# Where tiles start in on-chip memory: padding the shared region to multiples of 512 bytes

## The reference

```python
mod = (c_act @ w_ada[l] + b_ada[l]).reshape(B, N_SUBLAYERS, 3, D)
shift, scale, gate = mod[:, :, 0], mod[:, :, 1], mod[:, :, 2]

h = x * (1.0 + scale[:, 0, None, :]) + shift[:, 0, None, :]
y = _swiglu(h, ffn1_w_in[l], ffn1_w_out[l])          # 1024 -> 2 x 2816 -> 1024
x = _layernorm(ALPHA * x + 0.5 * gate[:, 0, None, :] * y, ...)

h = x * (1.0 + scale[:, 1, None, :]) + shift[:, 1, None, :]
proj = h @ w_in[l]
cq, ckv, k_rope_raw, u = jnp.split(proj, split_at, axis=-1)
attn = _mla(cq, ckv, k_rope_raw, positions, ...)     # 8 heads, chunk-causal
pooled = _multiscale_pool(u, pool_w[l], pool_b[l], pool_scale[l])
y = jnp.concatenate([attn, pooled], axis=-1) @ w_out[l]
x = _layernorm(ALPHA * x + gate[:, 1, None, :] * y, ...)
...                                                  # a second feed-forward like the first
```

## The kernel before

| tile | start | by 512 | by 64 | by 2,048 |
|---|---|---|---|---|
| h_hi, h_lo, x, w_hi, w_lo, raw, act_t, sums | 4,096 to 120,832 | 0 | 0 | 0 |
| ones_t, ones_d | 123,456; 123,968 | 64 | 0 | 576; 1,088 |
| gb | 124,576 | 160 | 32 | 1,696 |
| ada_first, a_hi1, a_hi2, u | 125,088 | 160 | 32 | 160 |
| w_hi_early, w_lo_early | 190,624; 198,816 | 160 | 32 | 160 |
| a_lo1, a_lo2 | 170,144 | 160 | 32 | 160 |
| c_act, ada_ring | 215,200; 219,296 | 160 | 32 | 160 |
| ckv | 133,536 | 416 | 32 | 416 |
| lat, cq, k_rope, poolw | 137,760; 170,528; 178,720; 180,768 | 32 | 32 | 544 |
| hn_hi, hn_lo | 183,200; 199,584 | 416 | 32 | 928 |
| Q, K, V, pt_even | 183,200; 191,392; 207,776; 215,968 | 416 | 32 | 928 |

## Time and profile before

### The profile page before, as it was taken

One profiled execution on the slowest core, in us unless ns is written; L12 is line 12 of the kernel. 1 busy time (PEld: TensorE's weight loads), 2 busy tenths in 40 slices (PEclk: granted clock), 3 DMA queues, 4 the chain that ended last, 5 costly groups with the idle time before them and its releaser, 6 DMA issues.

```text
span 992.9 us, 10623 instructions
## 1 busy us (share of the span) xinstructions
PE 956.1 (96%) x4130; PEld 761.7 (77%) x4130; DVE 509.4 (51%) x718; ACT 373.5 (38%) x546; POOL 241.8 (24%) x209
## 2 busy tenths in 40 slices
PE   4999999999999999999999999999999999999992
PEld 3788888888878887777766786888888888788881
DVE  5956767545456754767655477722322222234225
ACT  3743232342222332655484447532332323212213
POOL 0021111111107221328834363611111111052110
PEclk8899999999999999999999999999999999999996
DMA  9836565656653744113511112323232232223202
GB/s 363 330 106 207 180 207 191 191 185 197 201 174 124 246 145 128 53 64 106 127 43 43 43 64 83 101 93 106 88 103 92 100 106 80 96 80 97 78 17 85
DMA packets 37474, 127.20 MB, mean 128 GB/s; under 512 B 4016, under 2 KB 4144, under 8 KB 37424
## 3 DMA queue, kind: packets, MB, share of 16 engines
q1 hardware_dynamic: 37424, 126.52, 38.5%
HBM read 123.36 MB, written 2.10 MB: 126 GB/s over the span
## 4 chain that ended last, share of the span: by engine, by line
PE 94%; DVE 3%; ACT 2%; issue 1%; DMA 0%; SPq 0%; DVEq 0%; ACTq 0%
PE bank L549 28%; PE bank L550 28%; PE bank L551 28%; PE bank L854 2%; PE bank L831 1%; PE bank L657 1%; PE bank L620 1%; PE bank L621 1%; PE bank L597 1%; PE bank L612 1%; DVE x L1283 1%; PE bank L842 1%; DVE w_lo L933 0%; DMA x<-xT 0%; PE bank L586 0%
## 5 line engine op out<-in xcount | busy, mean ns | idle before, releaser
L933 DVE TENSOR_TENSOR w_lo<-raw,w_hi 128x1024 fp32r<-128x1024 f32 x159 | 217.3, 1373 | 301.8 <-ACT w_hi L925 301.3
L549 PE MATMUL bank<-h_hi,w_hi 128*128 128x512 f32 x730 | 286.4, 392 | 0.0
L551 PE MATMUL bank<-h_hi,w_lo 128*128 128x512 f32 x730 | 284.4, 390 | 0.0
L550 PE MATMUL bank<-h_lo,w_hi 128*128 128x512 f32 x730 | 284.3, 390 | 0.0
L925 ACT ACTIVATE w_hi<-raw 128x1024 fp32r<-128x1024 f32 x159 | 162.3, 1032 | 207.9 <-PE bank L551 206.8
L1661 POOL TENSOR_TENSOR a_lo<-act_t,a_hi 128x512 fp32r<-128x512 f32 x44 | 58.5, 1329 | 428.1 <-ACT a_hi L1009 428.1
L549 PEld LDWEIGHTS bank<-h_hi,w_hi 128*128 128x128 f32 x730 | 137.2, 188 | 29.3 <-issue 1.1
L551 PEld LDWEIGHTS bank<-h_hi,w_lo 128*128 128x128 f32 x730 | 137.2, 188 | 28.7
L550 PEld LDWEIGHTS bank<-h_lo,w_hi 128*128 128x128 f32 x730 | 137.2, 188 | 28.3 <-issue 0.5
L549 PE MATMUL bank<-a_hi,w_hi 128*128 128x512 f32 x352 | 141.1, 401 | 0.0
L551 PE MATMUL bank<-a_hi,w_lo 128*128 128x512 f32 x352 | 139.5, 396 | 0.0
(11 more groups left out here) (252 smaller groups left out, 1003.7 us busy)
## 6 DMA issues: line engine op xcount, KB each, us to landing
raw<-wunits SPq DMA_DIRECT2D x145, 512.0 KB, 3.2
ada_ring<-ada_w SPq DMA_DIRECT2D x56, 512.0 KB, 4.5
ada_first<-ada_w SPq DMA_DIRECT2D x16, 512.0 KB, 8.9
raw<-wunits SPq DMA_DIRECT2D x16, 384.0 KB, 2.9
x<-xT SPq DMA_DIRECT2D x4, 512.0 KB, 5.7
outT<-x SPq DMA_DIRECT2D x8, 256.0 KB, 2.0
K<-k_rope SPq DMA_DIRECT2D x2, 512.0 KB, 8.0
c_act<-c_rows SPq DMA_DIRECT2D x1, 512.0 KB, 8.0
```

The lines of the kernel that those rows point to most:

```text
L549: mm(out, lh, rh, start=first, stop=False)
L550: mm(out, lh, rl, start=False, stop=False)
L551: return mm(out, ll, rh, start=False, stop=last)
L933: nc.vector.tensor_tensor(lo, raw[:, slot, 0:width], hi.bitcast(F32), SUB).then_inc(s_lo, 1)
```

## The change

Three tiles that nothing uses are made longer or added, so that what is declared after them lies further on.

```diff
-        margin2 = sb("margin2", [P, 54])
+        margin2 = sb("margin2", [P, 142])
...
         ckv = sb("ckv", [P, KKV, PADW + TOK], F32, mix_ctx)
+        fit = sb("fit", [P, 32], F32, mix_ctx)
         lat = sb("lat", [P, 2 * KD, TOK], F32R, mix_ctx)
...
         inverse = sb("inverse", [P, STEPS], F32, mix_ctx)
+        fit2 = sb("fit2", [P, STEPS], F32, mix_ctx)
         proj_ctx = ExitStack()
```

## The result

| | before | after |
|---|---|---|
| median, four runs each on one chip | 993.85 us (993.32 to 994.58) | 983.32 us (983.16 to 984.38) |
| profiled execution, its span | 994.68, 992.9 | 983.47, 981.7 |
| ratio, 95% interval | | 0.9896 (0.9883 to 0.9908) |

A forecast was written before the change was run, and what follows sets the result against it. TensorE's matmul pace bounds the kernel; savings of 8.0 (a), 1.3 (hn), 1.2 (lat moving), 0.2 (V) and 0.3 (early weights) sum to 11.0 us, taking 994.68 to 983.7, stated as 983.5; range 981.5 to 986.5.

The forecast's parts named there:

- The bound: Whole kernel: TensorE, busy 956.1 of 992.9 us, sets the time by how often a matmul can start.
- The a matmuls: Down halves of both feed-forwards: 1,056 matmuls with a_hi or a_lo moving, each 7.6 ns shorter, 8.0 us.
- The early weights: At the start: 48 matmuls with the early weight tiles stationary, each 7.1 ns shorter, 0.3 us.
- hn, V, K and the first Q: Projection with hn moving, then lat moving for K and two heads' Q, stationary for V: together 1.8 us saved.
- Given back in part: Rival, 5%: weight supply or attention chain takes up the room, down halves run 1 ns short; 986.1 us.
- the supply of weights: Split weights must keep up as a unit of 24 matmuls shortens from 5.62 to 5.44 us.
- The second opening: Opening of the second feed-forward: 96 matmuls with lat moving, each 6.6 ns shorter, 0.6 us.
- The attention's fills: Attention loop: 72 matmuls with lat moving, 0.5 us, half counted because TensorE waits for others there.
- Transfers, VectorE, float32, at nothing: Moved DMA destinations, other engines' operands and float32 matmuls: no gain counted; bounds 1.6 us for DMA, 0.3 for float32.
- up to 1 us for the destinations: Start of the kernel: misaligned DMA rows pay an extra transaction, 133 beats for 128, 4%; not counted.
- A reading that fits: float32r matmuls: a moving row off a 64-byte line touches 33 lines instead of 32, giving 233.8 against 226.7 ns.
- the stationary operand counts too: Early weights at remainder 160 with aligned h moving: 8 steps take 233.8 ns each, so weight starts cost as well.

The follow-up runs named there:

- the kernel with the old destinations: Changed kernel with ada_first, x_tok, c_act, ada_ring, u back at 160 and ckv at 416 past a multiple of 512, float32r tiles kept at their new places: 983.38 us.
- the first experiment: Kernel before the change with its shared region 32 bytes further on, so every moving row starts on a multiple of 64 bytes: 992.31 us, ratio 0.9985.
- all at 32: Changed kernel with every float32r tile but gb at remainder 32 by 256 bytes, none on a 64-byte line: 983.84 us, ratio 0.9903.
- low tiles at 32: Changed kernel with every tile from h_hi to margin2 moved 32 bytes, the shared region kept aligned: 992.81 us, ratio 0.9993.

## Why the prediction was right, and where it was not

- **The bound.** Right: TensorE's pace sets the end, and the time won in each stage stands at the end unchanged through the up halves and the loop.
- **The a matmuls, 8.0 us.** 3.9 in each down half, 7.9.
- **The early weights, 0.3.** Their 48 steps fell from 233.2 to 227.5 ns on the mean, 0.3; the lead grows by 0.45 over that stretch, the rest beside them.
- **hn, V, K and the first Q, together 1.8.** 1.0. The step is as forecast (227.0 ns), but 0.45 us turned into the new wait at q_sum, and some 0.4 more was lacking, in small losses along the stretch that no run explains. "Given back in part" was a rival of its own; the forecast had nothing of it, and what I had named as the danger, the supply of weights, was not what came late: it was GpSimd's q_sum.
- **The second opening, 0.6.** 0.5, at 227.8 ns.
- **The attention's fills.** Half of 0.5 us was counted; the loop gave nothing.
- **Not foreseen:** 0.7 us from the race of VectorE and GpSimd at the entry of the loop, where I took nothing. It made up for what was lacking, so that the total of 10.5 by chance lies nearer to 11.0 than its parts do: without the race won the traces give 9.8. Who won in the executions without a trace isn't known; on the chip where the kernel after was measured once more, the medians are 994.23 and 984.08, 10.2 us apart.
- **Transfers, VectorE, float32, at nothing.** Right: for transfers and VectorE by the kernel with the old destinations, for float32 by the equal steps of V with pt_even and with u. By the Trainium skill (DMA: Bandwidth & Descriptors, How a descriptor splits into AXI transactions) the prediction estimated up to 1 us for the destinations; no such gain was measured. What that section describes are bytes fetched ahead of a descriptor's start, and here only destinations moved.

The forecast of the time came out, and by luck as far as its cause goes. The step that failed is the cause, "A reading that fits: a row of 2,048 bytes that starts on a 64-byte line touches 32 lines, one that starts inside a line 33". The numbers fitted to 0.2% and it was false: rows on 64-byte lines were slow (the first experiment) and rows inside lines fast (all at 32). So was the sentence that the stationary operand counts too, as a cost of its own. In its place stands: a matmul of this shape steps in 226.7 ns if moving and weight rows have the same remainder by 256, and in 229 to 238 ns if not. The forecast came out because the change makes both remainders 0, and the step of 226.7 ns was read from rows where both were 0 already. Where theories built on single starts had to forecast a kernel with both off, low tiles at 32, they gave 1,026 or 1,008 us, and it took 992.8. The float32r rows of before held only pairs with one operand at 0, and so could not separate the two. The Trainium skill (SBUF — State Buffer, Specifications (TRN2)) has a line of 16 bytes; if starts within such a line were all that counted, differences of 32, 64 or 160 would all be free, and they cost 2 to 8 ns each.

## What to carry to other kernels

Where TensorE is the bound and float32r matmuls of one shape run at two paces, print the address of each operand and compare moving with stationary by 256 bytes; make all of them equal, most simply 0. Look at pairs, not at tiles: moving one tile "into alignment" while its partner is off costs as much per matmul as the reverse (h alone 32 bytes off: 15.4 us, weights alone: 22.9 us, both: nothing in their stage). And a reading that matches a ratio to three digits is still to be tested with a run in which it and its neighbour disagree.

## What the runs showed of the hardware

- The pace of a 128 x 512 float32r matmul at full clock depends on the relative start of its two operands, and repeats after 256 bytes wherever that was tried (256 as 0, 320 as 64, 384 as 128; 160 and 416 alike): 226.7 ns at 0, 229 at 64, 231.7 at 16, 233 to 234 at most others, 237.9 at 4. Float32 matmuls of 256 to 512 columns show nothing of it at differences of 64, 128 and 192 (215 to 429 ns a step, as at 0). Other shapes and types weren't tried. That a load of 512 bytes per partition, hidden beside the stream, can slow the stream by 3% was not expected. Why, these runs don't show.
- Destinations that start at 160 or 0 by 512 bytes took transfers about equally fast (381 and 374 GB/s).
- VectorE's difference of 1,024 elements against GpSimd's of 512, started within 0.2 us: the first takes 1.2 to 1.3 us, the second 2.2 to 2.4, and VectorE is the first only if it leads by more than about 0.01 us; 0.07 was enough.
